# One-hot rows of eight tokens by one half-precision compare, in a product-key retrieval kernel

## The chip, the cores and the metric

The kernel runs on one core of a Trainium2 chip. The metric is the device time of one launch in microseconds (us). The engines are PE (TensorE: matmuls; PEld is its weight loads), DVE (VectorE), ACT (ScalarE), POOL (GpSimd) and SP (SyncE, which here only issues DMAs).

## The reference, cut to what matters

One encoder block on 1024 tokens of width 1024. The change lies in its last part, a retrieval with product keys (8 heads, 128 x 128 experts, the best 16 per head):

```
s = einsum('thpe,hpke->thpk', q, keys)          # two score rows of 128 per token and head
sv, si = top_k(s, 16)
cand = sv[:, :, 0, :, None] + sv[:, :, 1, None, :]
tv, ti = top_k(cand, 16)
eidx = (si0 * 128 + si1)[ti];  g = softmax(tv)
a = einsum('cd,ced->ce', x, utab[eidx])
out = einsum('ce,ced->cd', g * gelu(a), vtab[eidx])
```

## The kernel before, in words

The block runs as stages, each with its own set of engine programs; within a stage the engines meet only through semaphores, and the order of each engine's work is written out by hand. Three stages matter here.

**stage_select** picks the experts. For 6 of the 8 tiles of 128 tokens (the "dense" 768 tokens) PE turns three rows of 128 picks per token (first key number, second key number, gate share) into columns, and ACT copies them to `sel`, [128 picks, 3, 768 tokens]. Beside that PE computes `u @ utab.T` for 56 of the 128 expert rows (tiles), each as 48 matmuls of 384 columns in three float32 parts (`product3`, L79 to L81).

**stage_gates** does two things at once. It computes the other 72 tiles of `u @ utab.T` (`aps`; ACT puts them through gelu and stores them in `ahead`). And it scatters the gate shares into a dense table `gates[i, j, token]`. For a token, `second` is [128 picks, 128] with a one where the pick's second key number is j, and `first` is the same for i, times the share. One matmul of the two gives the token's 128 x 128 table. The share is kept as two half-precision parts, so there are two matmuls per token, 1536 in all (L1880). Tokens come in 192 groups of 4; the tables of a group fill one PSUM bank, which ACT copies out (`scatter_out`, L1899). In the program of PE a tile's 24 matmuls of the first half are followed by all groups of the tile but the last, and the second 24 by the last.

The one-hot rows are built per token by DVE from a half-precision row of column numbers, `iota`, as `tensor_scalar` compares: L1975 for `second`, L1980 for compare and share in one (twice, for tokens 0 and 1 of a group), L1977 for the bare compare of tokens 2 and 3, whose shares ACT then multiplies in (L1917, four per group, two groups ahead). There are four buffers, each for one group. DVE's program for a tile is: its groups (2 or 3), after each group one or two `dot`s (L1988, 1024 elements), and then `low` (L1993), which makes the low part of the next tile's `ut` and lets PE start that tile. The dots work on 256 expert rows that POOL gathers from DRAM into four slots (L1856); a slot is refilled when its dot is done. At the start SP loads the row of column numbers (L1838) and DVE prepares the shares (L1964 to L1968).

**stage_values** multiplies `ahead` by `gates`, splits the product and the rows of `vtab` into high and low parts, and accumulates 128 tiles of matmuls in groups of four (L79 to L81 with `va_` names). Its loads are issued by SP in program order (L2047 to L2062). `last_gates` are the semaphores of the three pieces in which the last block of `gates` is stored: rows 0 to 1, 2 to 7 and 8 to 127.

Of the kernel before, what the change touches and what calls it, by code (L numbers as in the profile page):

```python
# [8 lines left out]
F32 = mybir.dt.float32  # L9
F32R = mybir.dt.float32r  # L10
F16 = mybir.dt.float16
# [1536 lines left out]
SLOTS_G = 4  # L1548

# [10 lines left out]
def stage_select(nc, S, K, T):  # L1560
# [6 lines left out]
    with ctx:  # L1567
# [10 lines left out]
        iota = sb("iota", [P, TOPK])  # L1578
# [22 lines left out]
        def _(sp):  # L1601
            sp.dma_start(iota[:, :], T["iota"][0:TOPK].partition_broadcast(P)).then_inc(small, 16)
# [11 lines left out]
        def _(pool):  # L1614
# [10 lines left out]
            low(0, AT * KT)  # L1625

# [30 lines left out]
        def _(act):  # L1657
# [10 lines left out]
            def pair(i, dense):  # L1668
                for s in range(2):
# [29 lines left out]
        def _(dve):  # L1699
# [20 lines left out]
            def pair(i, dense):  # L1720
                for s in range(2):
# [24 lines left out]
                    for a in range(2):  # L1746
                        ch.link(v.tensor_tensor(hit[:, a, :, :], ab[:, a, :].unsqueeze(2).to_broadcast([P, PICKS, TOPK]),
                                                iota[:, :].unsqueeze(1).to_broadcast([P, PICKS, TOPK]), ALU.is_equal))
# [32 lines left out]
def stage_gates(nc, S, K, T):  # L1781
# [7 lines left out]
    with ctx:  # L1789
# [4 lines left out]
        iota32 = sb("iota32", [P, NK])  # L1794
        iota = sb("iota", [P, NK], F16)
        gh16 = sb("gh16", [P, DENSE], F16)
        gs = sb("gs", [P, 2, DENSE])
        first = sb("first", [P, 4, 2, G, NK], F16)
        second = sb("second", [P, 4, G, NK], F16)
# [10 lines left out]
        small, chain_s, f_ok, mm, act_out = (sem(n) for n in ("small", "chain", "f_ok", "mm", "act_out"))  # L1810
        shares_ok, hot_ok = sem("shares_ok"), sem("hot_ok")
# [6 lines left out]
        TURNS = 1  # L1818
        BY_ACT = (2, 3)
        TILES = BESIDE // TURNS  # L1820
        GROUPS = DENSE // G // TURNS
        ROWS = GATHERED * PICKS // TURNS
# [7 lines left out]

        def rows_after(b):
            return range(ROWS * b // GROUPS, ROWS * (b + 1) // GROUPS)

# [25 lines left out]
        def _(pe):  # L1859
            pe.sem_inc(mm, 4)  # L1860
            pe.sem_inc(a_mm, 4)
            for i in range(TURNS):
                for q in range(TILES):
                    n, s = TILES * i + q, q % 2
                    pe.wait_ge(ut_ok, n + 3)
                    todo = list(groups_of(q))
                    for h in range(2):
                        pe.wait_ge(gelu_ok, 2 * n + h + 1)
# [607 lines left out]
```

## Time and profile before

| | us |
|---|---|
| median of 3 runs | 4094.34 (4091.97 to 4097.99) |
| the profiled execution | 4094.17 |
| its span in the trace | 4092.4 |
| mean granted PE clock | 0.955 of full |

| engine | busy us | share of the span |
|---|---|---|
| PE | 3711.1 | 91% |
| DVE | 2666.7 | 65% |
| ACT | 1177.5 | 29% |
| POOL | 1195.0 | 29% |

The span runs from the first to the last instruction in the trace; the profiled execution's own time is 1.8 us more. Busy time of an engine is the union of its instructions' time. These are averages over stages with different limits: stage_gates lies at about 2150 to 2943 us of the span, stage_values behind it.

### The profile page before, as it was taken

What the parts mean: (1) busy time and instruction counts of PE and PEld (TensorE: products, weight loads), DVE (VectorE), ACT (ScalarE), POOL (GpSimd) and SP (SyncE); (2) the same over time, 40 slices, a digit from 0 to 9 for tenths busy, and PEclk for the clock granted to TensorE, in tenths of its full rate; (3) what the DMA queues carried; (4) which work ended last, traced back from release to release, by engine and by line L of the source; (5) the groups of instructions that cost most, each with busy time, mean ns of one, the idle gap of its engine ahead of it and who ended that gap; (6) DMA issues with size and microseconds to landing.
All of it is one profiled execution on the core that took longest, in us unless ns stands there. A gap on an engine that the chain in (4) does not pass through costs nothing. (4 is left out here: it accounts for less than half of the span.)

```text
span 4092.4 us, 54523 instructions
## 1 busy us (share of the span) xinstructions
PE 3711.1 (91%) x19170; PEld 3240.0 (79%) x19170; DVE 2666.7 (65%) x5849; ACT 1177.5 (29%) x2129; POOL 1195.0 (29%) x797
## 2 busy tenths in 40 slices
PE   5879899998887889899998999989679999999997
PEld 2579878886666778899998888888658888888875
DVE  4563033222555521699989999999767777777777
ACT  1110122221115221222335555556422222222220
POOL 1132112211332011233334343344333333333340
PEclk9789999998898989999999999999989999999998
DMA  4651212124545122333338999999988778888883
GB/s 174 262 194 36 88 59 74 71 76 155 201 159 185 67 86 78 115 129 121 131 112 276 310 327 311 327 315 325 309 283 291 286 282 293 290 291 294 290 292 112
DMA packets 502708, 826.52 MB, mean 202 GB/s; under 512 B 289175, under 2 KB 309911, under 8 KB 496440
## 3 DMA queue, kind: packets, MB, share of 16 engines
q1 hardware_dynamic: 111848, 370.03, 25.7%
q0 software_dynamic: 84096, 318.80, 21.4%
q10 hardware_dynamic: 306576, 135.28, 13.4%
q8 instruction: 105, 1.72, 0.2%
q14 instruction: 83, 0.68, 0.0%
HBM read 679.31 MB, written 144.70 MB: 201 GB/s over the span
## 5 line engine op out<-in xcount | busy, mean ns | idle before, releaser
L79 PE MATMUL va_fps<-va_vt_h,va_c_h 128*128 128x512 f32 x1536 | 608.1, 396 | 69.7 <-DVE va_vt_l L2210 36.0
L80 PE MATMUL va_fps<-va_vt_l,va_c_h 128*128 128x512 f32 x1536 | 605.7, 394 | 0.0
L81 PE MATMUL va_fps<-va_vt_h,va_c_l 128*128 128x512 f32 x1536 | 604.9, 394 | 0.0
L2088 POOL DMA_INDIRECT va_rows<-in_vtab,k_pick x256 | 396.5, 1549 | 657.9 <-DVE k_big L2234 572.8
L79 PE MATMUL ga_aps<-k_u_h,k_ut_h 128*128 128x384 f32 x1152 | 404.1, 351 | 13.9 <-DVE k_ut_l L1993 10.2
L79 PEld LDWEIGHTS va_fps<-va_vt_h,va_c_h 128*128 128x128 f32 x1536 | 293.4, 191 | 134.8 <-issue 38.4
L81 PE MATMUL ga_aps<-k_u_h,k_ut_l 128*128 128x384 f32 x1152 | 391.2, 340 | 0.0
L80 PE MATMUL ga_aps<-k_u_l,k_ut_h 128*128 128x384 f32 x1152 | 390.8, 339 | 0.0
L2234 DVE SCALAR_TENSOR_TENSOR k_big<-va_rows,va_coef,k_big 128x1024 f32<-128x1024 f32 x254 | 320.2, 1282 | 56.3 <-DMA va_rows<-in_vtab,k_pick 55.7
L80 PEld LDWEIGHTS va_fps<-va_vt_l,va_c_h 128*128 128x128 f32 x1536 | 293.6, 191 | 61.2
L81 PEld LDWEIGHTS va_fps<-va_vt_h,va_c_l 128*128 128x128 f32 x1536 | 293.1, 191 | 61.5
L1917 ACT ACTIVATE ga_first<-ga_first,ga_gs 128x128 f16<-128x128 f16 x768 | 245.6, 391 | 323.1 <-DVE ga_first L1977 323.1
L79 PE MATMUL se_aps<-k_u_h,k_ut_h 128*128 128x384 f32 x896 | 301.4, 336 | 15.5 <-POOL k_ut_l L1619 15.5
L2175 ACT ACTIVATE va_vt_h<-va_vt 128x1024 fp32r<-128x1024 f32 x128 | 135.3, 1057 | 577.4 <-PE va_fps L81 389.0
L80 PE MATMUL se_aps<-k_u_l,k_ut_h 128*128 128x384 f32 x896 | 300.8, 336 | 0.0
L81 PE MATMUL se_aps<-k_u_h,k_ut_l 128*128 128x384 f32 x896 | 300.6, 336 | 0.0
L1619 POOL TENSOR_TENSOR k_ut_l<-k_ut,k_ut_h 128x1024 fp32r<-128x1024 f32 x57 | 148.8, 2610 | 359.0 <-ACT k_ut_h L1666 359.0
L79 PEld LDWEIGHTS ga_aps<-k_u_h,k_ut_h 128*128 128x128 f32 x1152 | 220.8, 192 | 16.4 <-DVE k_ut_l L1993 12.2
L1856 POOL DMA_INDIRECT k_big<-in_urows,k_pick x128 | 171.3, 1338 | 193.1 <-DVE k_big L1988 174.5
L1856 POOL DMA_INDIRECT ga_rows<-in_urows,k_pick x128 | 145.8, 1139 | 279.7 <-DVE ga_rows L1988 264.9
L80 PEld LDWEIGHTS ga_aps<-k_u_l,k_ut_h 128*128 128x128 f32 x1152 | 220.7, 192 | 0.0
L81 PEld LDWEIGHTS ga_aps<-k_u_h,k_ut_l 128*128 128x128 f32 x1152 | 220.0, 191 | 0.0
(296 smaller groups left out, 8144.6 us busy)
## 6 DMA issues: line engine op xcount, KB each, us to landing
k_ut<-in_utab SPq DMA_DIRECT2D x129, 512.0 KB, 6.0
va_vt<-in_vtab SPq DMA_DIRECT2D x128, 512.0 KB, 6.9
va_c<-scratch_ahead SPq DMA_DIRECT2D x128, 384.0 KB, 3.4
va_wt<-scratch_gates SPq DMA_DIRECT2D x128, 384.0 KB, 5.1
hy_tab<-in_tab POOLq DMA_DIRECT2D x64, 512.0 KB, 4.8
scratch_ahead<-ga_gelu_a ACTq DMA_DIRECT2D x72, 384.0 KB, 5.7
sp_wada<-in_w_ada SPq DMA_DIRECT2D x24, 1024.0 KB, 8.6
scratch_gates<-ga_wide ACTq DMA_DIRECT2D x32, 768.0 KB, 12.1
```

Source lines behind the costliest of these rows:

```text
L79: nc.tensor.matmul(out, w[0], x[0], start=first, stop=False)
L80: nc.tensor.matmul(out, w[0], x[1], start=False, stop=False)
L81: return nc.tensor.matmul(out, w[1], x[0], start=False, stop=last)
L1619: nc.gpsimd.tensor_tensor(ut_l[:, s, :, :], ut[:, s, :, :], ut_h[:, s, :, :].bitcast(F32), ALU.subtract).then_inc(ut_ok, 1)
L1856: nc.gpsimd.indirect_dma_start(got[q % SLOTS_G], None, T["urows"], picked(K, q)).then_inc(got_in[q % SLOTS_G], 16)
L1917: last = nc.scalar.activation(first[:, b, part, t, :], first[:, b, 0, t, :], ACT.Copy, scale=gs[:, part, at:at + 1])
L2088: nc.gpsimd.indirect_dma_start(got[:, q % SLOTS_G, :], None, vrows, picked(K, q)).then_inc(got_in[q % SLOTS_G], 16)
L2175: nc.scalar.activation(vt_h[:, s, t, :], vt[:, t % 2, :], ACT.Copy).then_inc(vt_hi, 1)
L2234: v.scalar_tensor_tensor(out=sums[:, n, :], in0=got[:, k, :], scalar=share, in1=sums[:, n, :], op0=ALU.mult, op1=ALU.add).then_inc(row_use ...
```

## The change

In stage_select the first two rows of the turned picks go to `at16`, in half precision, and the share to `sel`, which is now [128, 768]. The column numbers 0 to 127 are loaded there once, and POOL writes them out as `iota16`, [128, 128 columns, 8 tokens], each number eight times in a row. stage_gates uses that: a batch is 8 tokens, `first` and `second` are stored as [columns, tokens], and DVE compares a whole batch in one `tensor_tensor` of 1024 elements for `first` and one for `second` (`hits`), and then multiplies in the two parts of the shares with two more (`weigh`, now on DVE). ACT no longer takes part. There are three buffers, each for one batch. PE's 1536 matmuls are the same in number and order, but read `first[:, b, part, :, t]` and `second[:, b, :, t]`: 128 half-precision numbers in steps of 8 elements, 16 bytes. DVE works up to two batches ahead of the tile.

In stage_values SP no longer loads `x1` at the start, and no longer waits for the third piece of the last gates before the loads of tiles 2 to 7; DVE waits for all three pieces before its first `turn` instead; POOL starts its gathers after two tiles are split.

```diff
@@ stage_select, gpsimd and scalar
+            pool.wait_ge(small, 16)
+            nc.gpsimd.tensor_copy(K["iota16"][:, :, :], K["iota"][:, :].unsqueeze(2).to_broadcast([P, NK, BATCH]))
...
-                    nc.scalar.activation(K["sel"][:, :, bass.ds((n - GATHERED) * P, P)],
-                                         tps[:, :].rearrange("p (a t) -> p a t", t=P), ACT.Copy).then_inc(t_ok, 1)
+                    at = bass.ds((n - GATHERED) * P, P)
+                    nc.scalar.activation(K["at16"][:, :, at], tps[:, 0:2 * P].rearrange("p (a t) -> p a t", t=P), ACT.Copy)
+                    nc.scalar.activation(K["sel"][:, at], tps[:, 2 * P:3 * P], ACT.Copy).then_inc(t_ok, 1)
@@ stage_gates
-        first = sb("first", [P, 4, 2, G, NK], F16)
-        second = sb("second", [P, 4, G, NK], F16)
+        SETS = 3
+        share16 = sb("share16", [P, 2, DENSE], F16)
+        first = sb("first", [P, SETS, 2, NK, BATCH], F16)
+        second = sb("second", [P, SETS, NK, BATCH], F16)
...
-            sp.dma_start(iota32[:, :], T["iota"][0:NK].partition_broadcast(P)).then_inc(small, 16)
@@ tensor
-                                    last = nc.tensor.matmul(ps[:, e, t * NK:(t + 1) * NK], second[:, e, t, :],
-                                                            first[:, e, part, t, :], start=part == 0, stop=part == 1)
+                                last = nc.tensor.matmul(ps[:, m % 4, t * NK:(t + 1) * NK], second[:, b, :, m * G % BATCH + t],
+                                                        first[:, b, part, :, m * G % BATCH + t], start=part == 0, stop=part == 1)
@@ scalar
-            def weigh(m):
...
-                        if m + AHEAD < BLOCKS * BLOCK:
-                            weigh(m + AHEAD)
@@ vector
-            def one_hot(m, b):
-                dve.wait_ge(mm, m + 1)
...
+            def hits(m):
+                if m >= SETS:
+                    dve.wait_ge(mm, 4 + BATCH // G * (m - SETS + 1))
+                b = m % SETS
+                v.tensor_tensor(first[:, b, 0, :, :], K["iota16"][:, :, :], of_batch(at16[:, 0, :], m), ALU.is_equal).then_inc(hot_ok, 1)
+                v.tensor_tensor(second[:, b, :, :], K["iota16"][:, :, :], of_batch(at16[:, 1, :], m), ALU.is_equal)
+
+            def weigh(m):
+                dve.wait_ge(hot_ok, m + 1)
+                b = m % SETS
+                for part in (1, 0):
+                    last = v.tensor_tensor(first[:, b, part, :, :], first[:, b, 0, :, :], of_batch(share16[:, part, :], m), ALU.mult)
+                last.then_inc(f_ok, 1)
...
+            for n in range(TILES):
+                for m in batches_of(n):
+                    if m:
+                        hits(m)
+                    for j in rows_after(m):
+                        dot(j)
+                    if m:
+                        weigh(m)
+                low(1 - n % 2, n + 1)
@@ stage_values, sync
-                sp.dma_start(x1[:, n, :], rows(S["x1"], order[n])).then_inc(x1_in[n], 16)
...
-            sp.wait_ge(K["last_gates"][1], 16)
-            sp.wait_ge(K["last_gates"][2], 16)
...
+            sp.wait_ge(K["last_gates"][1], 16)
+            for n in range(2, 8):
+                load(n % 2, n)
+            sp.wait_ge(K["last_gates"][2], 16)
@@ gpsimd and vector
+            pool.wait_ge(c_lo, 4)
...
+            for k in range(3):
+                dve.wait_ge(K["last_gates"][k], 16)
```

On DVE in the middle of stage_gates there stood, for a group of four tokens, its dots, and the start of the next group (`ga_first` and `ga_second` are the one-hot rows, `k_big` and `ga_rows` the slots of gathered rows):

```order
L1975 TENSOR_SCALAR ga_second<-ga_iota,k_sel 128x128
L1980 TENSOR_SCALAR ga_first<-ga_iota,k_sel,ga_gs 128x128 x2
L1975 TENSOR_SCALAR ga_second<-ga_iota,k_sel 128x128
L1980 TENSOR_SCALAR ga_first<-ga_iota,k_sel,ga_gs 128x128 x2
L1975 TENSOR_SCALAR ga_second<-ga_iota,k_sel 128x128
L1977 TENSOR_SCALAR ga_first<-ga_iota,k_sel 128x128
L1975 TENSOR_SCALAR ga_second<-ga_iota,k_sel 128x128
L1977 TENSOR_SCALAR ga_first<-ga_iota,k_sel 128x128
L1988 SCALAR_TENSOR_TENSOR k_big,k_dots<-k_big,k_u_row 128x1024 x2
```

Now, for a batch of eight tokens and the `low` behind it:

```order
L1957 TENSOR_TENSOR ga_first<-k_iota,k_at 128x1024
L1958 TENSOR_TENSOR ga_second<-k_iota,k_at 128x1024
L1977 SCALAR_TENSOR_TENSOR k_big,k_dots<-k_big,k_u_row 128x1024 x2
L1977 SCALAR_TENSOR_TENSOR ga_rows,k_dots<-ga_rows,k_u_row 128x1024
L1964 TENSOR_TENSOR ga_first<-ga_first,ga_share 128x1024 x2
L1982 TENSOR_TENSOR k_ut_l<-k_ut,k_ut_h 128x1024
```

Ten short instructions per four tokens have become four long ones per eight; the dots now stand between the compares and the products.

On SP at the start of stage_values (`va_c`, `va_wt` and `va_vt` are the tiles of `ahead`, `gates` and `vtab`) there stood:

```order
L2048 DMA va_c<-scratch_ahead 128x768
L2049 DMA va_vt<-in_vtab 128x1024
L2050 DMA va_x<-scratch_x 128x1024
L2048 DMA va_c<-scratch_ahead 128x768
L2049 DMA va_vt<-in_vtab 128x1024
L2050 DMA va_x<-scratch_x 128x1024
L2053 DMA va_wt<-scratch_gates 128x768 x2
L2068 UNCONDITIONAL_BRANCH
```

Now:

```order
L2039 DMA va_c<-scratch_ahead 128x768
L2040 DMA va_vt<-in_vtab 128x1024
L2039 DMA va_c<-scratch_ahead 128x768
L2040 DMA va_vt<-in_vtab 128x1024
L2043 DMA va_wt<-scratch_gates 128x768 x2
L2047 DMA va_c<-scratch_ahead 128x768
L2048 DMA va_wt<-scratch_gates 128x768
L2050 DMA va_vt<-in_vtab 128x1024
```

Two loads are gone from ahead of the first gates, and the loads of tiles 2 to 7 stand ahead of the loop, at whose entry (the branch) SP waited for the last two pieces.

## Rows read from the trace of the kernel before

**Rows 1.** Windows (us; busy time and instructions per engine, granted PE clock, DMA share, GB/s)

```profile
1700.00:2100.00 400.00, 400.00 (x2315) 399.82 (x2314) 374.81 (x1415) 119.10 (x169) 126.53 (x48) 1.00 0.36 129
2160.00:2940.00 780.00, 711.00 (x4947) 678.86 (x4948) 732.24 (x2490) 455.65 (x1168) 313.13 (x252) 0.99 1.08 314
```

**Rows 2.** Waits, 2160 to 2940: who waited for whom, us in total, times, longest

```profile
PE ga_ps L1880 <- ACT ga_first L1917: 61.9, 44, 3.7
...
PE ga_aps L79 <- DVE k_ut_l L1993: 10.2, 9, 2.9
DVE k_big L1988 <- DMA k_big<-in_urows,k_pick: 8.9, 8, 2.9
```

**Rows 3.** Timeline of DVE, one group of four tokens: start, us

```profile
2407.93 0.25 DVE L1975 TENSOR_SCALAR ga_second<-ga_iota,k_sel 128x128 f16<-128x128 f16 x1
...
2409.80 1.23 DVE L1988 SCALAR_TENSOR_TENSOR ga_rows<-ga_rows,k_u_row 128x1024 f32<-128x1024 f32 x1
2410.95 0.09 DVE L1988 DVE_READ_ACCUMULATOR ga_rows<-ga_rows,k_u_row 128x1 f32 x1
```

**Rows 4.** Instruction groups, 2160 to 2940: busy us, mean ns, idle before

```profile
L1917 ACT ACTIVATE ga_first<-ga_first,ga_gs 128x128 f16<-128x128 f16 x764 | 244.4, 391 | 311.5 <-DVE ga_first L1977 311.5
...
L1993 DVE TENSOR_TENSOR k_ut_l<-k_ut,k_ut_h 128x1024 fp32r<-128x1024 f32 x71 | 87.2, 1228 | 37.0 <-ACT k_ut_h L1894 36.8
```

**Rows 5.** Timeline of PE: one group's eight scatter matmuls

```profile
2407.64 0.62 PE L1880 MATMUL ga_ps<-ga_first,ga_second 128*128 128x128 f16 x8
```

**Rows 6.** One line's instructions, durations min/median/max: L1880, L981, L1312

```profile
L1880 PEld LDWEIGHTS ga_ps<-ga_first,ga_second x1536: 95/98/153, 2160.6 to 2942.8; 128*128 128x128 f16 x192
L1880 PE MATMUL ga_ps<-ga_first,ga_second x1536: 218/220/315, 2160.6 to 2942.8; 128*128 128x128 f16 x192
...
L981 PEld LDWEIGHTS hy_ps<-k_ident,k_big x64: 194/209/227, 1000.5 to 1125.3; 128*128 128x128 f32 x64
...
L1312 PEld LDWEIGHTS ou_tps<-k_ident,ou_row x64: 138/140/231, 1358.7 to 1434.0; 128*128 128x128 f32 x64
```

**Rows 7.** DVE groups of the whole span: short, strided and plain copies and sums

```profile
L560 DVE COPY k_qk<-pj_tps 128x128 f32<-128x128 f32 x80 | 22.8, 388 | 3.0 <-PE pj_tps L490 3.0
...
L1086 DVE TENSOR_TENSOR k_big<-k_big 128x512 f32<-128x512 f32 x16 | 11.1, 693 | 0.5
...
L1110 DVE TENSOR_TENSOR hy_prod<-hy_prod 128x512 f32<-128x512 f32 x8 | 5.5, 685 | 0.0
...
L557 DVE COPY k_qk<-pj_tps 128x256 f32<-128x256 f32 x8 | 3.3, 416 | 0.0
```

**Rows 8.** Timeline of DVE at the start of stage_gates

```profile
2153.89 0.23 DVE L1964 CAST ga_iota<-ga_iota 128x128 f16<-128x128 f32 x1 [15.67 <-DMA ga_iota<-in_iota]
```

**Rows 9.** Timelines of SP, DVE and PE at the start of stage_values

```profile
2951.60 1.05 SPq L2053 DMA_DIRECT2D va_wt<-scratch_gates  x2
2973.94 0.34 SPq L2059 DMA_DIRECT2D va_c<-scratch_ahead  x1
...
2965.97 0.96 DVE L2202 TENSOR_TENSOR va_c<-va_c,va_wt 128x768 f32<-128x768 f32 x1 [18.43 <-DMA va_wt<-scratch_gates]
...
2970.04 0.77 PE L79 MATMUL va_fps<-va_vt_h,va_c_h 128*128 128x512 f32 x1 [27.00 <-DVE va_vt_l L2210]
```

**Rows 10.** Windows around that start, as rows 1

```profile
2950.00:2960.00 10.00, 0.00 (x0) 0.00 (x0) 0.00 (x0) 1.06 (x1) 1.80 (x2) 0.50 1.00 368
2980.00:2990.00 10.00, 5.45 (x18) 4.04 (x18) 6.04 (x7) 3.69 (x4) 0.00 (x0) 0.83 0.73 253
```

**Rows 11.** DMA issues, 2940 to 3000: engine, KB each, us to landing

```profile
scratch_gates<-k_big ACTq DMA_DIRECT2D x1, 2880.0 KB, 28.8
```

**Rows 12.** DMA, 2160 to 2940: total, and one gather's time to landing

```profile
DMA packets 300766, 244.61 MB, mean 314 GB/s; under 512 B 250328, under 2 KB 250328, under 8 KB 300692
...
k_big<-in_urows,k_pick POOLq DMA_INDIRECT x126, 7.5
```

More of the change, by code:

```diff
@@ L1548 @@
 SLOTS_G = 4
+BATCH = 8
 def dense_half(h):
@@ new lines, in _ @@
+            for n in range(TILES):
+                s, todo = n % 2, list(groups_of(n))
+                pe.wait_ge(ut_ok, n + 3)
+                for h in range(2):
+                    pe.wait_ge(gelu_ok, 2 * n + h + 1)
+                    cut = dense_half(h)
+                    for k in range(KT):
+                        last = product3(nc, aps[:, 2 * s + h, 0:DH], (ut_h[:, s, k, :], ut_l[:, s, k, :]),
+                                        (u_h[:, k, cut], u_l[:, k, cut]), k == 0, k == KT - 1)
+                    last.then_inc(a_mm, 1)
+                    for m in (todo[:-1], todo[-1:])[h]:
+                        pe.wait_ge(f_ok, m * G // BATCH + 1)
+                        pe.wait_ge(act_out, m + 1)
+                        b = m * G // BATCH % SETS
+                        for t in range(G):
+                            for part in range(2):
+                                last = nc.tensor.matmul(ps[:, m % 4, t * NK:(t + 1) * NK], second[:, b, :, m * G % BATCH + t],
+                                                        first[:, b, part, :, m * G % BATCH + t], start=part == 0, stop=part == 1)
+                        last.then_inc(mm, 1)
@@ L1971, in one_hot @@
-            def one_hot(m, b):
-                dve.wait_ge(mm, m + 1)
-                for t in range(G):
-                    at = slice(m * G + t, m * G + t + 1)
-                    v.tensor_scalar(second[:, b, t, :], iota[:, :], K["sel"][:, 1, at], None, ALU.is_equal)
-                    if t in BY_ACT:
-                        last = v.tensor_scalar(first[:, b, 0, t, :], iota[:, :], K["sel"][:, 0, at], None, ALU.is_equal)
-                        continue
-                    for part in range(2):
-                        v.tensor_scalar(first[:, b, part, t, :], iota[:, :], K["sel"][:, 0, at],
-                                        gs[:, part, at], ALU.is_equal, ALU.mult)
-                last.then_inc(hot_ok, 1)
@@ new lines, in weigh @@
+            def weigh(m):
[4 more added lines that the diff above has]
+                last.then_inc(f_ok, 1)
+            hits(0)
+            ch.link(v.tensor_scalar(scaled[:, :], scaled[:, :], GATE_SCALE, None, ALU.mult))
+            ch.link(v.tensor_copy(share16[:, 0, :], scaled[:, :]))
+            ch.link(v.tensor_tensor(share16[:, 1, :], scaled[:, :], share16[:, 0, :], ALU.subtract))
@@ L1986, in dot @@
+            weigh(0)
+            def dot(j):
+                k, turn = j % SLOTS_G, j // SLOTS_G
                 dve.wait_ge(got_in[k], 16 * (turn + 1))
@@ L1994, in low @@
                                 ALU.subtract).then_inc(ut_ok, 1)
-            for i in range(TURNS):
-                for q in range(TILES):
-                    for b in groups_of(q):
-                        one_hot(GROUPS * i + b, b % 4)
-                        for j in rows_after(b):
-                            dot(i, j)
-                    low(1 - q % 2, TILES * i + q + 1)
+            for n in range(TILES):
+                for m in batches_of(n):
[6 more added lines that the diff above has]
+                low(1 - n % 2, n + 1)
 def stage_values(nc, S, K, T, out):
```

94 lines of the change are left out of this document (29 added, 65 removed).

## The prediction

> **What bounds the kernel now.** I read the windows first. In stage_select PE is busy for all of 400 us [rows 1]: 2315 matmuls, 0.173 us from one 384-column matmul to the next. In stage_gates it is busy for 711 of 780 us, and DVE for 732. So PE has some 69 us to win there. The waits say for what: 61.9 us for the one-hot rows of a group, which ACT finishes last, and 10.2 us for the low part of the next tile [rows 2]. ACT itself stood idle for 311.5 us waiting for DVE's compares [rows 4], so ACT is only the last link: DVE sets the pace. DVE's time for a tile, 780 / 72 = 10.83 us, can be added up. A group of four tokens takes 2409.80 - 2407.93 = 1.87 us of short compares, a dot 2410.95 - 2409.80 = 1.15 us [rows 3]. A tile has 2.67 groups, 3.56 dots and one `low`, which lasts 1.23 us and holds the engine for about as long as a dot [rows 4]: 4.99 + 4.09 + 1.15 = 10.2 us, and DVE's idle time of 780 - 732 = 48 us over 72 tiles is the other 0.67.
>
> PE's own need is 711 / 72 = 9.9 us per tile. It comes out of the pieces too: 48 x 0.173 = 8.3, and the other 1.6 us are 2.67 groups of 0.6 us each: eight scatter matmuls, 0.057 us from start to start ((0.62 - 0.22) / 7) [rows 5, 6], and the change-over.
>
> **The change, part by part.**
>
> *DVE in stage_gates.* Per eight tokens 3.74 us of short compares go, and four tensor_tensor of 1024 half-precision elements come. The trace has none such. Upper bound: as long as 1024 float32 elements, 1.15 us each. Lower bound, and the nearer row: as long as 512 float32 elements, which are the same number of bytes; they take 0.685 us alone [rows 7], 0.61 back to back if the 0.08 us by which a `low` overlaps its follower holds here too. I take 0.61, by bytes. A tile has 1.33 batches: 5.33 x 0.61 = 3.3, with dots and `low` 8.5 us, below PE's 9.9. At 1.15 it is 6.1 and 11.4 us. It crosses PE's 9.9 at 0.87 us per operation. The Trainium skill (Vector Engine (DVE) Microarchitecture Reference, section 5.1) says that a tensor_tensor whose operands all have two bytes and innermost step 1 takes two elements per cycle, also where one row is read again and again; no row here shows it.
>
> *ACT.* 768 activations go, 245 us off an engine that was busy for 456 [rows 1, 4]. Nothing waits longer for it; what gains is the 61.9 us of PE's wait.
>
> *PE.* Same matmuls, same order, but both operands are read in 16-byte steps. No row has that. The nearest: L981 loads 128 float32 columns in steps of 8 bytes (every second token) and takes 209 ns; L1312, the same transpose without steps, 140 [rows 6]. That is 0.54 ns more per column. A half-precision load takes only 98, so its reading goes another way, and loads hide under the matmul before them. How the moving read, which sets the 0.057, reacts, no row tells. Bounds: nothing, and the price of a new 16-byte line for each column. With 8-byte steps two columns share a line, and cost 2 x (0.417 + 0.54) = 1.9 ns (0.417 is one column at the full 2.4 GHz); one line per column would be 128 x 1.9 = 244 ns per matmul. For: DVE's copy of 128 elements into lines of their own (L560, steps of 1 KB) takes 388 ns where 256 plain ones take 416, about 1 ns more per element, and an 8-byte step costs DVE nothing (L1086 with steps, 693; L1110 without, 685) [rows 7]. Against: those are another engine's, and writes. I take nothing as the likeliest, because the two-byte operand asks for half of the bytes per column of the row that was slowed and I see no matmul spaced wider by a step; but this is the term on which everything hangs, and both ends stay. The Trainium skill (Advanced Engine Details and Errata, Memory Cachelines) speaks against the change: a 16-byte line must be hit at least twice to absorb the access time, and a new line at each access is penalised. Of its first half the trace disagrees for PE's loads: two hits per line were already slower, 209 against 140.
>
> *What PE wins.* With DVE at 8.5 us per tile the 61.9 us go; I leave the 10.2 for `low`. **-61.9 us.**
>
> *Start of stage_gates.* The load of the column numbers kept DVE idle until 2153.89 [rows 8]; it is gone, and the first batch is ready before PE's first 24 matmuls end. What PE loses by it lies mostly inside the 61.9, so I count nothing here. POOL writes the column numbers out after its last `low` in stage_select, under PE's last tile of 8.3 us: 1024 elements, for which its operations there took 126.53 / 48 = 2.6 us [rows 1]. Uncovered it would cost just that. ACT's second copy at the end of each dense tile is of 128 columns; its copies of 128 columns take 0.39 us [rows 4], once on the path to the next stage: nothing.
>
> *Start of stage_values.* PE stood for 27.0 us until the first tile was split, because the gates of that tile, issued at 2951.6, came at 2966.0; then again because the loads of tile 2, held by the last piece of the gates (2880 KB, 28.8 us), were issued only at 2973.9 [rows 9, 11]. The two loads of x1 and four gathers, 512 KB each, 3.1 MB, no longer share the way; at the 368 GB/s moved there [rows 10] they are 8.5 us. So the first tile comes some 8 us earlier. Tile 2's loads then leave about 2961, land within 7, and its part of PE's second stop (4.6 us of 2980 to 2990 [rows 10]) mostly goes: 3 more. The price if SP's loads collide instead: the 4.6 us stay and the first tile wins 5. **-11 us**, between -5 and -20. The gathers start later but are used only behind four tiles, and DVE's wait for the pieces ends before that.
>
> Sum against the profiled execution: 4094.2 - 61.9 - 11 = **4021 us**; its time is within 0.2 us of the median of the runs.
>
> **The rivals.** Each is 4021 plus a price.
>
> 1. *A step costs PE as in the row of 8 bytes.* 128 x 0.957 = 122 ns instead of 57, 1536 times: +100, **4121 us**. PE becomes the bound of its own accord, at 11.3 us per tile, and DVE's relief is worth nothing.
> 2. *Each column is a line of its own*, 244 ns: +287, **4308 us**, slower. The place is PE in stage_gates, and the spacing of the scatter matmuls decides: the gain is gone from 0.105 us on ((4094 - 4021) / 1536 + 0.057). The Trainium skill's rule on 16-byte lines, cited above, would give this case.
> 3. *DVE takes one element per cycle.* 11.4 us per tile instead of 10.2, nothing of the 61.9 is won: 4094.2 + 72 x 0.6 (over today's 10.83) - 11 = **4126 us**. Against it: the short compares already run 128 elements in 0.16 us.
> 4. *The transfers set it.* 244.6 MB in 718 us are 341 GB/s; the core moved 368 at the start of stage_values [rows 10, 12], so there is room. A slot's round is 780 / 64 = 12.2 us now and would have to be 11.2; issue 1.24 (313 / 252), landing 7.5 and dot 1.15 make 9.9, and DVE waited only 8.9 us for such a slot [rows 1, 2, 12]. If landings stretch and half is lost: **4052 us**.
>
> **How the numbers follow.** A measurement of this kernel tells a difference from none at about 0.2%, 8 us. Chances: forecast 0.48, and 0.05 for a step that costs less than the limit above; rival 1 0.22; rival 2 0.17; rival 3 0.04; rival 4 0.04. Faster: 0.48 + 0.05 + 0.04 = 0.57. Rival 1 touches "the same" where the step costs a little less than its row (102 to 110 ns), 0.08 of its 0.22. Slower: 0.14 + 0.17 + 0.04 = 0.35. The range goes down to 3990 (the 10.2 us of `low` and the larger gain at stage_values, 9 more, and some clock) and up to 4130, over rivals 1, 3 and 4; it leaves out rival 2. The forecast's own range is 3990 to 4050.
>
> **What would show it.** Right: the eight scatter matmuls of a group last 0.62 us as before; PE is busy for all but some 15 us of stage_gates, which lasts about 720; L1957, L1958 and L1964 take about 0.69 each and DVE is idle for 15% of the stage, waiting for buffers; ACT is busy for under 30% of it; from PE's last scatter matmul to its first matmul of stage_values there are 19 us instead of 27. Wrong: a group of eight that lasts 1.1 us (rival 1) or 2 us (rival 2), a load of L1882 well over 98 ns; tensor_tensor of 1.2 us (rival 3); waits of DVE for the gathered rows that make up tens of us (rival 4). If the second stop of PE in stage_values stays, the term of 11 us is wrong in its second part.

## The result, and the profile after

The changed kernel takes **4288.07 us** (median of 4 runs, 4285.92 to 4289.18) where the kernel before takes 4094.22 us beside it: the ratio is **1.0472, 95% interval 1.0454 to 1.049**. It is slower by 194 us. The forecast was 4021 us with a range up to 4130; rival 2 had said 4308.

The profiled execution (span 4286.3 us) says where. stage_gates, from its first matmul to the start of its last scatter matmul, goes from 2148.6 to 3148.1: 999.5 us where before it was 792.9. What lies behind that is 11.4 us shorter (1138.2 instead of 1149.6 to the end of the span). +206.6 - 11.4, and 1.3 us by which stage_gates starts earlier, make the 194.

The windows of stage_gates, with the columns of [rows 1]:

```profile
2160.00:3130.00 970.00, 958.50 (x4848) 818.96 (x4847) 609.07 (x957) 254.39 (x397) 357.78 (x251) 0.97 0.94 251
```

PE is busy for 99% of it, DVE for 63% instead of 94%, ACT for 26%; the same bytes now take longer, so the transfers fell from 314 to 251 GB/s. The waits of the same stretch say it too, against [rows 2]:

```profile
DVE ga_first L1957 <- PE ga_ps L1882: 350.1, 92, 8.7
...
PE ga_aps L79 <- DVE k_ut_l L1982: 11.5, 1, 11.5
```

The 61.9 us for one-hot rows are gone, and DVE now waits 350 us for PE. What PE does with the time stands in the scatter matmuls' own records and in the timeline of one batch, against [rows 5, 6]:

```profile
L1882 PEld LDWEIGHTS ga_ps<-ga_first,ga_second x1536: 142/146/168, 2154.5 to 3147.8; 128*128 128x128 f16 x192
L1882 PE MATMUL ga_ps<-ga_first,ga_second x1536: 405/413/442, 2154.5 to 3148.1; 128*128 128x128 f16 x192
```
```profile
2605.32 3.94 PE L1882 MATMUL ga_ps<-ga_first,ga_second 128*128 128x128 f16 x16
```

A load takes 146 ns instead of 98, a matmul 413 instead of 220, and sixteen of them start (3.94 - 0.41) / 15 = 0.235 us apart instead of 0.057. 1536 x 0.178 us are 273 us; some 60 us of waits that PE no longer has come off. DVE's share went as forecast: 1024 half-precision elements take the time of 512 float32 elements, 0.685 us alone (0.685 in [rows 7] too), and 0.61 us back to back (1.29 - 0.68; the pair of 1.29 us is in e1's timeline below).

```profile
L1964 DVE TENSOR_TENSOR ga_first<-ga_first,ga_share 128x1024 f16<-128x1024 f16 x190 | 122.4, 685 | 0.0
...
L1957 DVE TENSOR_TENSOR ga_first<-k_iota,k_at 128x1024 f16<-128x1024 f16 x94 | 65.1, 692 | 350.1 <-PE ga_ps L1882 350.1
L1958 DVE TENSOR_TENSOR ga_second<-k_iota,k_at 128x1024 f16<-128x1024 f16 x94 | 64.3, 685 | 0.0
```

The start of stage_values went as forecast as well (timelines, against [rows 9]): SP issues tile 2's loads 10 us after it asked for the first tiles' gates, where it had been 22. PE's gap is 18.42 us, not 27.00, and its second stop (4.55 us before) is 2.40.

```profile
3155.47 1.01 SPq L2043 DMA_DIRECT2D va_wt<-scratch_gates  x2
3165.73 0.33 SPq L2047 DMA_DIRECT2D va_c<-scratch_ahead  x1
...
3166.89 0.76 PE L79 MATMUL va_fps<-va_vt_h,va_c_h 128*128 128x512 f32 x1 [18.42 <-DVE va_vt_l L2204]
3179.53 0.50 PE L79 MATMUL va_fps<-va_vt_h,va_c_h 128*128 128x512 f32 x1 [2.40 <-DVE va_vt_l L2204]
```

### The profile page after: what moved, and what is told of

Read it like the earlier page. It is cut to its first block and busy times, and to the rows that moved or that the text cites. A ratio compares the mean times of both kernels' runs of the same rounds, so it can differ in the third digit from the quotient of the medians.

```text
span 4286.3 us, 52188 instructions
## 1 busy us (share of the span) xinstructions
PE 3975.4 (93%) x19170; PEld 3392.1 (79%) x19170; DVE 2544.9 (59%) x4311; ACT 980.1 (23%) x1367; POOL 1241.9 (29%) x798
## 5 line engine op out<-in xcount | busy, mean ns | idle before, releaser
L79 PE MATMUL ga_aps<-k_u_h,k_ut_h 128*128 128x384 f32 x1152 | 423.9, 368 | 15.2 <-DVE k_ut_l L1982 11.5
L1882 PE MATMUL ga_ps<-ga_first,ga_second 128*128 128x128 f16 x1536 | 387.2, 415 | 0.0
L1882 PEld LDWEIGHTS ga_ps<-ga_first,ga_second 128*128 128x128 f16 x1536 | 211.8, 147 | 127.6 <-issue 22.6
L1957 DVE TENSOR_TENSOR ga_first<-k_iota,k_at 128x1024 f16<-128x1024 f16 x96 | 66.5, 692 | 361.3 <-PE ga_ps L1882 350.1
L1860 POOL DMA_INDIRECT ga_rows<-in_urows,k_pick x128 | 177.0, 1383 | 350.7 <-DVE ga_rows L1977 314.9
L1860 POOL DMA_INDIRECT k_big<-in_urows,k_pick x128 | 187.4, 1464 | 255.9 <-DVE k_big L1977 226.3
```

Of the source, the lines that this page charges most:

```text
L79: nc.tensor.matmul(out, w[0], x[0], start=first, stop=False)
L1860: nc.gpsimd.indirect_dma_start(got[q % SLOTS_G], None, T["urows"], picked(K, q)).then_inc(got_in[q % SLOTS_G], 16)
L1882: last = nc.tensor.matmul(ps[:, m % 4, t * NK:(t + 1) * NK], second[:, b, :, m * G % BATCH + t], first[:, b, part, :, m * G % BATCH + t], ...
L1957: v.tensor_tensor(first[:, b, 0, :, :], K["iota16"][:, :, :], of_batch(at16[:, 0, :], m), ALU.is_equal).then_inc(hot_ok, 1)
```

## The experiments

Each is the kernel before or the changed one with the edit shown. e1, e2, e3 and e12 read other numbers than the one-hot rows, and e7 and e10 store the gates at another place in DRAM than the one they are read from, so these six compute a wrong result; counts and shapes stay. Stage lengths are taken as above, from the first matmul of stage_gates to the start of its last scatter matmul, in one profile each. PE's busy time and clock are those of the window 2160 to 2850.

| kernel | time, us | ratio to before, 95% interval | stage_gates | PE busy of 690 us | clock |
|---|---|---|---|---|---|
| before | 4094 | 1 | 792.9 | 632.2 | 0.98 |
| changed | 4288 | 1.0454 to 1.049 | 999.5 | 678.5 | 0.97 |
| e1, both reads plain | 4094 | 0.9996 to 1.002 | 803.5 | 624.7 | 0.96 |
| e2, moving read plain | 4100 | 1.0016 to 1.0047 | 813.6 | 641.0 | 0.95 |
| e3, loaded read plain | 4282 | 1.0456 to 1.0491 | 999.1 | 681.5 | 0.95 |
| e12, e3 with a 32-byte step | 4282 | one run | 999.2 | 682.4 | 0.96 |
| e4, pairs (4-byte step) | 4088 | 0.9996 to 1.002 | 807.3 | 631.7 | 0.96 |
| e5, low part early | 4060 | 0.9913 to 0.9961 | 767.8 | 651.3 | 0.97 |
| e6, dots spread | 4045 | 0.9875 to 0.9924 | 765.4 | 649.8 | 0.97 |
| e11, e6 with an 8-byte step | 4076 | 0.9956 to 0.9984 | 791.6 | 688.1 | 1.00 |
| e7, e4 with long packets | 4095 | 1.0005 to 1.004 | 810.5 | 622.3 | 0.95 |
| e10, e6 with long packets (two runs) | 3997 | 0.9741 to 0.9812 | 707.2 | 687.3 | 1.00 |
| e9, tile's store from SP | 4048 | 0.9884 to 0.9927 | 761.8 | 655.3 | 0.97 |
| e13, gates' stores from SP | 4041 | 0.986 to 0.9899 | 754.0 | 656.4 | 0.98 |
| e14, gates' stores from both | 4041 | 0.9862 to 0.9903 | 758.5 | 657.2 | 0.97 |
| e8, before, values' order alone | 4079 | 0.9973 to 1.0002 | 793.8 | 629.9 | 0.99 |
| e15, e6 with gates in blocks | **3986** | 0.975 to 0.9787 | 707.1 | 686.7 | 1.00 |
| e16, before, gates in blocks | 4062 | 0.9932 to 0.997 | 780.0 | 635.5 | 0.99 |

The kernel before took 4071 to 4105 us over the runs beside these; the ratios are to its runs on the same chip. In the profiles stage_gates starts anywhere between 2138 and 2157 us, also where all that lies ahead of it is the same, so of a difference between two profiles only what lies inside the stage that an edit touches is put down to it.

### Which read, and what a step costs: e1, e2, e3, e12

My theory: PE pays for a new 16-byte line in each column, in which of its two reads was open, and with plain reads the rest of the prediction comes true. The rivals stand in each expectation.

```diff
 # e1: both operands (j = the token's place in the batch); e2: the second only; e3: the first only
-second[:, b, :, j]
+second[:, b, 16 * j:16 * j + 16, :].rearrange("p n t -> p (n t)")
-first[:, b, part, :, j]
+first[:, b, part, 16 * j:16 * j + 16, :].rearrange("p n t -> p (n t)")
 # e12: e3, and the moving operand with every second column, out of both parts
-first[:, b, part, :, j]
+first[:, b, :, :, :].rearrange("p a (n z) t -> p a n (z t)", z=2)[:, :, :, j]
```

> The scatter matmuls read, out of the same buffers, 128 half-precision numbers that lie side by side (16 columns of 8 tokens) instead of every eighth number. They are not the one-hot rows, so the gates are other numbers; counts, shapes, order and waits are those of the changed kernel. Theory 'step' (the 16-byte step of PE's two reads is the whole loss; the rest of the prediction holds): the sixteen matmuls of a batch back at 0.057 us from start to start (0.62 us for eight), loads 98 ns, stage_gates some 720 us, time 4015 to 4035. Rival 'memory' (PE's reads are slow because DVE writes 1024-element rows beside them, or because the 2 KB of a batch lie together): spacing stays near 0.23 us and the time at 4288. Rival 'rest': the spacing is back, but DVE or the transfers then bound the tile at more than 9.9 us: 4050 to 4126.

> Only the moving operand is read side by side; the loaded one keeps its 16-byte step (the gates are other numbers again). Theory 'each pays' (load and moving read each pay a line per column and go one after the other): half of the 0.17 to 0.18 us that the spacing grew remains, spacing 0.14 us, time 4021 + 0.085 x 1536 = 4150. Theory 'moving' (only the moving read is on the path, a load hides under the matmul before it): spacing 0.057 to 0.07 us, time 4020 to 4040. Theory 'longer' (both take the same and overlap, the longer one counts): spacing stays at 0.23 us, 4288.

> The mirror of the run before: only the loaded operand is read side by side, the moving one keeps its 16-byte step. 'Each pays': spacing 0.14 us, 4150 us. 'Moving': spacing stays at 0.23 us, 4288 us, and the load's record goes from 146 back to 98 ns. 'Longer': also 4288. With the run before, the three theories give 4150 and 4150, 4030 and 4288, 4288 and 4288.

> The kernel of e3 (changed kernel, loaded operand side by side) with the moving operand read in steps of 32 bytes instead of 16: 64 columns from each of the two parts of a batch, so other gates. Theory 'a line per column' (16 bytes already give each column a line of its own; more can't cost more): spacing 0.224 us as in e3, 4280 us. Theory 'by the step': 0.4 us or more, 4550 or more.

The scatter matmuls' records of e1, e2 and e3, one fence each, then one group of eight of e3 and one of e12:

```profile
L1883 PEld LDWEIGHTS ga_ps<-ga_first,ga_second x1536: 96/98/103, 2151.9 to 2950.7; 128*128 128x128 f16 x192
L1883 PE MATMUL ga_ps<-ga_first,ga_second x1536: 218/220/232, 2151.9 to 2950.8; 128*128 128x128 f16 x192
```
```profile
L1883 PEld LDWEIGHTS ga_ps<-ga_first,ga_second x1536: 143/148/172, 2146.1 to 2953.8; 128*128 128x128 f16 x192
L1883 PE MATMUL ga_ps<-ga_first,ga_second x1536: 222/226/281, 2146.1 to 2953.8; 128*128 128x128 f16 x192
```
```profile
L1883 PEld LDWEIGHTS ga_ps<-ga_first,ga_second x1536: 97/116/118, 2149.0 to 3141.4; 128*128 128x128 f16 x192
L1883 PE MATMUL ga_ps<-ga_first,ga_second x1536: 387/405/408, 2149.0 to 3141.6; 128*128 128x128 f16 x192
```
```profile
2511.85 1.98 PE L1883 MATMUL ga_ps<-ga_first,ga_second 128*128 128x128 f16 x8
```
```profile
2510.99 2.01 PE L1883 MATMUL ga_ps<-ga_first,ga_second 128*128 128x128 f16 x8
```

It is the **moving read**. With it plain, the matmul is back at 226 ns although its load still takes 148; with only the load plain, the matmul stays at 405 and the kernel at 4282 us. The stepped load costs 50 ns in its own record, under the matmuls, and some 6 us of the whole (4100 against 4094 in e2 and e1, 4288 against 4282 in the changed kernel and e3; the stage of e2 is 10 us longer than that of e1). A 32-byte step costs what 16 bytes cost, within some 2% ((1.98 - 0.41) / 7 = 0.224 us in e3, (2.01 - 0.41) / 7 = 0.229 in e12), so it isn't the distance but the line per column that is paid.

But e1 and e2 also show a **second failed step**. With the reads mended the time should have been 4021; it is 4094 and 4100. PE's busy time is back, and so is its idle time. The waits of e1 and one place of its timelines (PE, DVE; 2160 to 2940):

```profile
DVE ga_first L1958 <- PE ga_ps L1883: 109.2, 44, 5.4
PE ga_aps L79 <- DVE k_ut_l L1983: 76.8, 24, 14.5
DVE ga_rows L1978 <- DMA ga_rows<-in_urows,k_pick: 42.0, 23, 3.9
```
```profile
2525.64 0.69 PE L79 MATMUL ga_aps<-k_u_h,k_ut_h 128*128 128x384 f32 x1 [5.05 <-DVE k_ut_l L1983]
...
2522.01 1.23 DVE L1978 SCALAR_TENSOR_TENSOR ga_rows<-ga_rows,k_u_row 128x1024 f32<-128x1024 f32 x1 [3.91 <-DMA ga_rows<-in_urows,k_pick]
2523.16 0.08 DVE L1978 DVE_READ_ACCUMULATOR ga_rows<-ga_rows,k_u_row 128x1 f32 x1
2523.16 1.29 DVE L1965 TENSOR_TENSOR ga_first<-ga_first,ga_share 128x1024 f16<-128x1024 f16 x2
2524.37 1.22 DVE L1983 TENSOR_TENSOR k_ut_l<-k_ut,k_ut_h 128x1024 fp32r<-128x1024 f32 x1
```

PE waits 5.05 us for the next tile's low part; DVE does it last in a tile, behind a dot product that waited 3.91 us for its gathered row. DVE is idle for a fifth of the stage and late all the same. In the changed kernel PE is slow enough for everybody, and only one such wait shows, 11.5 us, at the start.

### Pairs, and the order of DVE's work: e4, e5, e6, e11

A layout of four pairs of tokens keeps DVE's single compare and gives PE steps of 4 bytes:

```diff
 # e4
-first = sb("first", [P, SETS, 2, NK, BATCH], F16)
-second = sb("second", [P, SETS, NK, BATCH], F16)
+first = sb("first", [P, SETS, 2, BATCH // STEP, NK, STEP], F16)      # STEP = 2
+second = sb("second", [P, SETS, BATCH // STEP, NK, STEP], F16)
-second[:, b, :, j], first[:, b, part, :, j]
+second[:, b, j // STEP, :, j % STEP], first[:, b, part, j // STEP, :, j % STEP]
 # e5: e4, and
     hits(m)
+    if m == batches_of(n)[0]: low(1 - n % 2, n + 1)
     for j in rows_after(m): dot(j)
     weigh(m)
-low(1 - n % 2, n + 1)
 # e6: compare, low, dot, compare, dot, product, dot, product: one dot behind each, as far as there are dots
 # e11: e6 with STEP = 4
```

> The same one compare for eight tokens, but the buffers hold pairs of tokens: [four pairs, 128, 2], so PE reads in steps of 4 bytes, four columns to 16 bytes. By the row of 8-byte steps of before (0.54 ns more per column of a load), halved for half the step: 0.27 x 128 = 35 ns more per matmul, +54, 4075 us. If what counts is only whether a 16-byte line is hit once, the step costs nothing: 4021. If any step sends a read down another way: 0.23 us, 4288. For DVE the innermost run is then 2 elements: it takes 0.69 us as now if length of the run doesn't matter, 1.15 or more if it does, and then DVE bounds the tile at 11.4 us or more: 4126 and up. The Trainium skill (Advanced Engine Details and Errata, Memory Cachelines) says that a line has to be hit at least twice; by that rule this kernel pays nothing for its steps.

> In e1 and e4 PE no longer waits for the one-hot rows but for the next tile's low part: 70 to 74 us in 22 to 25 waits, where the kernel before had 62 + 10. The kernel of e4 with one thing moved: DVE computes the next tile's low part right behind the first compare of a tile instead of behind all its batches. Theory 'order' (the low part is late because it stands behind a compare that waits for a buffer of PE's and behind three dot products that wait for gathered rows): the wait falls from 74 to under 20 us and the time from 4088 to 4025 to 4045. Theory 'transfers' (at 314 to 319 GB/s the DMA engines are full in stage_gates in every version, so whatever gets rid of one wait finds another): the waits change their names, the stage stays at 800 us, time 4080 to 4090.

> As the run before, and the two or three dot products of a batch no longer stand together: one behind each of the batch's four compares and products. Theory 'bursts' (a gathered row's place is freed three at a time, POOL then issues three gathers one behind the other, 1.3 us each, and the last lands too late): DVE's waits for gathered rows fall from 50 to 60 us to under 15, as with the even spacing of the kernel before (8.9), and the time is 10 to 30 us below e5, 4015 to 4030. Theory 'transfers': DVE's waits for rows stay above 40 us and the time is within 5 us of e5.

> The kernel of e6 with quads of tokens instead of pairs: PE reads in steps of 8 bytes, two columns to 16 bytes. The nearest row of before, a load of 128 float32 columns in steps of 8 bytes, took 69 ns more than one without. Theory 'any line hit twice is free' (that row is slow for its four-byte numbers): spacing 0.057 us, load 98, time as e6, 4045. Theory 'by the step' (the price grows with the step between 4 bytes, where e4 pays nothing, and 16, where it is 0.17 us): spacing 0.09 to 0.12 us, +50 to +100 us on PE, time 4060 to 4130. The Trainium skill (Advanced Engine Details and Errata, Memory Cachelines) has two hits per line as enough.

One group of eight of e4, then of e11:

```profile
2506.49 0.65 PE L1884 MATMUL ga_ps<-ga_first,ga_second 128*128 128x128 f16 x8
```
```profile
2509.01 1.11 PE L1884 MATMUL ga_ps<-ga_first,ga_second 128*128 128x128 f16 x8
```

**4 bytes cost PE nothing** (0.060 us apart), **8 bytes 0.116 us** ((1.11 - 0.30) / 7), 16 and 32 bytes 0.22 to 0.24. Per column that is 0.47, 0.9 and 1.8 ns: one 16-byte line in about 1.8 ns, shared by as many columns as lie in it. With four in a line that comes to 0.45 ns, as much as a column takes in a plain read (0.057 us / 128), so nothing is left to pay. The Trainium skill (Advanced Engine Details and Errata, Memory Cachelines) says that at least two hits on a line absorb the access. For one hit the measurement agrees. For two it doesn't: e11 pays 0.056 us for each of 1536 matmuls, 86 us of PE's time; its stage is only 26 us longer than e6's, because PE no longer has e6's waits (38 us of 690) and its clock is 1.00 instead of 0.97. DVE does not mind runs of two elements: 0.69 us as before.

e4 ends at 4088, the time of the kernel before, so it isn't the step alone. e5 and e6 move nothing but DVE's order. PE's wait for the low part (2160 to 2850) goes 66.3, 36.3, 37.0 us; DVE's waits for gathered rows 49.0, 74.8, 33.9. The order was worth 40 us of stage. The spreading won 15 us of time by the medians, but the stage that it touches is only 2 us shorter, so its worth isn't shown. Both are less than I had expected (PE's wait under 20 us, the rows' under 15). What is left of PE's wait has changed its cause. ACT's and DVE's waits of e6, and a piece of ACT's timeline:

```profile
ACT k_ut_h L1898 <- issue: 136.6, 32, 8.0
DVE k_ut_l L1993 <- ACT k_ut_h L1898: 100.9, 28, 8.1
PE ga_aps L79 <- DVE k_ut_l L1993: 37.0, 14, 5.6
```
```profile
2458.34 0.45 ACTq L1912 DMA_DIRECT2D scratch_gates<-k_big  x1
...
2464.19 7.20 ACTq L1930 DMA_DIRECT2D scratch_ahead<-ga_gelu_a  x1
2471.49 1.06 ACT L1898 ACTIVATE k_ut_h<-k_ut 128x1024 fp32r<-128x1024 f32 x1 [6.73 <-issue]
```

ACT issues a piece of the gates in 0.45 us and then stands for 7.20 us at the issue of the next store; its rounded copy, DVE's low part and PE stand behind it.

### Queue or transfers: e7, e9, e10, e13, e14

Every piece of the gates is 4096 runs of 192 bytes in DRAM (32 columns of 128 partitions; the 12,288 in e9's expectation was a slip). Is it these packets, and do they fill a queue or the DMA engines? In e7 and e10 SP also waits for all three last pieces before it loads the first gates; in e13 and e14 it issues its pieces between its loads of the next tiles (`k_ut`).

```diff
 # e7: e4 and e10: e6, the same bytes in another place
-act.dma_start(S["gates"].rearrange("i j t -> j i t")[:, lo:hi, block * TW:(block + 1) * TW], ...)
+act.dma_start(S["gates"].rearrange("i j t -> i (j t)")[:, at + lo * TW:at + hi * TW].rearrange("p (i t) -> p i t", t=TW), ...)
 # e9: e6, the store of the finished tile from SP
-act.dma_start(S["ahead"][n + FIRST], gelu_a[:, a, :])
+sp.dma_start(S["ahead"][bass.ds(n + FIRST, 1)][0], gelu_a[:, a, :])
 # e13: e6, the gates' pieces from SP; e14: every second piece
-act.dma_start(S["gates"]..., wide...)
+sp.dma_start(S["gates"]..., wide...)
```

> The kernel of e4, but the gates are stored with each partition's 32 x 48 numbers side by side (6 KB) instead of in 32 pieces of 192 bytes; the same bytes, in another place, so the values are summed with other gates. stage_values waits for all three last pieces before its first gates are read, which costs some 15 to 20 us once. It tests the transfers alone: their queue (q10 of the page) holds 47.7% of the 16 engines' time in stage_gates for 73 of 243 MB. Theory 'transfers': gathers land in 6 us instead of 7.8, PE's wait for the low part falls from 74 to under 25 us, stage_gates from 800 to 740 us; the time 4045 to 4055. Theory 'order': the wait stays above 50 us, the stage at 780 to 800 us, the time at 4090 to 4105.

> The kernel of e6 with the gates stored in 6 KB pieces as in e7 (another place, so other gates are summed; stage_values waits for all three last pieces). In e7 ACT's issues never lasted more than 0.35 us, but DVE was late by its order. Theory 'queue': with the order mended and short packets gone, both waits are gone: ACT for 'issue' under 10 us, PE for the low part under 10 us, stage_gates 25 to 45 us shorter than in e6; the whole 3990 to 4025, some 15 of it for the wait for the pieces. Theory 'order is all': nothing more to win, PE still waits some 40 us, 4045 to 4060.

> In e6 PE still waits 42.6 us for the next tile's low part, because DVE waits 103 us for ACT's rounded copy, and ACT waits 144 us for nothing but its own sequencer: its issue of the store of a finished tile took up to 8.9 us (median 2.3; in the kernel before 0.34). The kernel of e6 with that store issued by SyncE instead, between its loads of the next tiles. Theory 'queue' (the issue stands behind the 12,288 short packets of a stored piece of gates in ScalarE's own queue, and everything behind it on ScalarE is late): ACT's waits for 'issue' fall under 20 us, PE's for the low part under 10, the granted clock of the stage rises from 0.97 to 0.99, time 3985 to 4010. Theory 'transfers' (the issue is slow because the 16 DMA engines are full): SyncE's issues become as slow, PE's waits stay at 35 us or more, time 4035 to 4050.

> The kernel of e6 with all pieces of the gates (but the last block's) issued by SyncE, so that ScalarE issues only the store of the finished tile. In e6 and e9 ScalarE's own issues blocked it for 100 to 144 us, whichever store stood second; in e10, with long packets, for 5. Theory 'queue' (what blocks is that ScalarE waits at its issue while its queue is full; the transfers themselves have room): ScalarE's waits for 'issue' fall under 15 us, SyncE's issues of a piece last up to 10 us and cost nothing, PE's waits for the low part fall from 42.6 under 15 us, time 4005 to 4025. Theory 'transfers' (the 192-byte packets fill the 16 engines, whoever issues them): ScalarE waits instead for a block's stores before it writes the next one, or DVE for gathered rows; PE's waits stay above 30 us, 4040 to 4055.

> As the run before, but every second piece from SyncE and the others from ScalarE. Theory 'queue': two queues are each half as full, no issue of either lasts over 1 us, a piece lands in 10 to 16 us; PE's waits for the low part under 10 us, time 4000 to 4020, a little better than e13. Theory 'transfers': as e6 within 5 us, 4040 to 4050.

e7 alone would have misled: long packets took the DMA share from 1.06 to 0.86 and won nothing, because DVE's order held PE at the same place (67.7 us of wait). With the order mended, e10 loses PE's wait but for 2.2 us and is 58 us shorter in the stage than e6. So the two causes lay one behind the other: from e4 on, the order alone won 40 us of the stage, the packets alone nothing, both together 100.

The remedy of "queue", another issuing engine, failed in three runs. In e9 the block moved on to the gates' own issues on ACT (up to 9.9 us), in e13 to SP's loads (first row below), for which ACT then waited (second row), and in e14 both engines were held, ACT for up to 11.4 us at the tile's store and SP for up to 6.3 at a load; all three end at 4041 to 4048, as e6.

```profile
L1847 SPq DMA_DIRECT2D k_ut<-in_utab x71: 328/6373/14481, 2148.0 to 2868.9; - x71
```
```profile
ACT k_ut_h L1915 <- DMA k_ut<-in_utab: 101.2, 32, 8.5
```
```profile
2160.00:2850.00 690.00, 656.43 (x4574) 633.01 (x4573) 565.28 (x894) 226.39 (x375) 274.23 (x238) 0.98 1.10 331
```

With DVE's order mended and short packets, e5, e6, e9, e13 and e14 have a DMA share of 1.10 to 1.11 (the third row is e13's; the share sums the packets' times, so it can pass 1); e10 and e15, with long ones, 0.95 to 0.96. That they move 354 to 356 GB/s and the others 326 to 331 says no more than the stages' lengths, since the bytes are the same. The Trainium skill (DMA: Bandwidth & Descriptors, Rules for kernel authors) says that spreading transfers over issuing engines brings no bandwidth; e13 and e14 agree.

So it is shown that the short packets cost e6 its 58 us, and that moving them between ACT and SP doesn't help. It is not shown that they fill the 16 engines. The traces speak rather for the hold at the issue: what was held was always on an engine that itself issued short packets (SP's longest issue in e9, which issues none there, is 0.63 us; ACT's in e13 is 0.40), and in all these runs something urgent stands behind it on that engine. The gathers of the same stretch hardly feel the packets: in the median they land in 7.2 to 7.9 us in e4, and in 6.7 to 7.5 in e7. A run in which an engine issues the short packets and nothing that anybody waits for was not made.

### A version with the right result: e15, and the parts alone: e8, e16

```diff
 # e15: e6, and e16: the kernel before, both with
-dram("gates", (NK, NK, DENSE))
+dram("gates", (DENSE // 48, NK, NK, 48))
-act.dma_start(S["gates"].rearrange("i j t -> j i t")[:, lo:hi, block * TW:(block + 1) * TW], ...)
+act.dma_start(S["gates"][block, :, lo:hi, :], ...)
-sp.dma_start(wt[:, s, :], S["gates"][bass.ds(n, 1)][0])
+sp.dma_start(tile_of(wt, s), S["gates"].rearrange("b j i t -> i j b t")[bass.ds(n, 1)][0])
 # e8: the kernel before with the change's stage_values alone
```

> e13 and e14 stayed at 4041 whichever queue carried the short packets: the 16 DMA engines are full with them. This is the kernel of e6 with the gates laid out in DRAM as [block of 48 tokens, j, i, token]: the same values, stored in pieces of 6 KB per partition and, in stage_values, read in packets of 192 bytes. Theory 'transfers': stage_gates becomes as in e10, some 36 us shorter than in e6 (708 us, clock 1.00); the short packets' time, 22% of 16 engines over 710 us, moves to stage_values (14% of its 1137 us, where the share is 0.80), which stays under 1. If it hides there: 4000 to 4015. Rival: the loads of gates in stage_values land later (5 us become 8 or more), its tiles wait, 20 us or more are given back: 4025 to 4060.

> The kernel before with this other layout of the gates alone. There DVE's and ACT's one-hot rows bound the tile, not the transfers. If that is so, stage_gates gains nothing (PE still waits some 60 us for the rows): 4085 to 4095 with a little more or less at stage_values. If short packets already held it back: 4050 to 4070.

> The kernel before, with the third part of the change alone: the order of loads at the start of stage_values, the gathers behind four tiles, DVE's waits for the last pieces. By the prediction's term and by the changed kernel (PE's gap 18.4 us instead of 27.0, no second stop of 4.6) it is worth 11 us: 4094 to 4083. If the gap closed only because stage_gates ended otherwise, it stays at 4094.

```profile
2160.00:2850.00 690.00, 686.72 (x4889) 664.21 (x4889) 602.44 (x954) 249.72 (x400) 290.32 (x250) 1.00 0.95 354
2950.00:3950.00 1000.00, 978.26 (x4291) 808.00 (x4290) 767.53 (x721) 217.58 (x239) 365.91 (x236) 0.99 0.87 284
```

e15 takes **3986 us, 2.3% less than the kernel before**. stage_gates is at PE's own need (x4889 in 686.7 us, one wait of 2.2). The short packets are now read in stage_values, where the share rises from 0.81 (e6) to 0.87 and PE loses nothing (978 us busy of 1000, e6 973). It is 14 us below the range that I expected. The stage came out at the 708 us of the expectation, but that is 58 us less than in e6 and not the 36 that I had put into the sum. Part of it is the clock, 1.00 instead of 0.97. PE's records show this as busy time: 649.80 / 4512 = 0.1440 us a matmul in e6, 686.72 / 4889 = 0.1405 here.

e16 was a miss: I expected nothing, it won 0.5% (19 us by the medians; its profile is 13 us shorter in stage_gates and 14 behind it, and another 11 us ahead of it, which the edit doesn't touch). PE's wait for the rows stayed (54.5 us of 690, before 53.5), so DVE sets that kernel's pace as read; but PE's wait for the low part, 7.4 us there before, is gone. The last piece of the gates (2880 KB) lands in 10.1 us instead of 28.8; how the 14 us behind stage_gates come about I did not follow up.

e8: the time doesn't settle it (0.9973 to 1.0002, centre -5 us). In its trace the gap is 19.90 us instead of 27.00, the second stop 0.36 instead of 4.55, and what lies behind stage_gates is 7.7 us shorter (1141.9 instead of 1149.6).

## Why the prediction was wrong

*What bounds the kernel now* was right as far as it went: DVE sets the pace, PE's own need is 9.9 us per tile. e15 runs at 707.1 / 72 = 9.8.

*DVE in stage_gates*: right. 0.61 us per operation by bytes. The Trainium skill (Vector Engine (DVE) Microarchitecture Reference, section 5.1) has two elements per cycle for it; the 685 ns, as for half as many float32 elements, agree.

*PE*: **the step "I take nothing as the likeliest" failed, and by it the verdict.** The bound was good: a line per column, worked out as 0.244 us from the transpose's load, measured 0.235. So was rival 1's: 0.122 at 8 bytes, measured 0.116. That my price came so near is in part luck: it was worked out from a float32 load, and this kernel's own half-precision load at the same 16-byte step lasts 146 ns, not 244. The reason I gave for "nothing", that a two-byte operand asks for half of the bytes per column, counts bytes where these runs show that lines count. The row of the 8-byte step (209 against 140 ns) was the only one that I had of PE's own reads with a step; it was slowed, and nothing spoke for 16 bytes being better. Its price belonged in the sum, and "nothing" among the rivals.

*What PE wins*: **the step "with DVE at 8.5 us per tile the 61.9 us go" failed too**, and would have cost the forecast by itself: 4094 (e1) instead of 4021. The wait for the one-hot rows went, and where 10.2 us of wait for the low part had been there were now 76.8 (e1, 2160 to 2940). It was an argument from averages. Eight tokens at once make DVE's work lumpy: a compare that waits for a buffer of PE's (109 us), then three dot products one behind the other whose rows come back singly, then the low part on which PE stands. I left the 10.2 us of `low` as they were and did not ask what stands ahead of it. Rival 4 was right that the transfers would matter, but not how: the same bytes went at 356 GB/s in long packets (e10), and it was the 192-byte packets that cost. That its 4052 lies where the kernels with mended order ended (4041 to 4060) is luck.

*ACT*: the 245 us went, and nothing waited for them: right.

*Start of stage_gates*: the load is gone, but PE stood 11.5 us for the second tile's low part, which DVE does behind the first tile's batches; I had counted nothing.

*Start of stage_values*: right. 11.4 us where 11 were forecast; the gap 18.42 where 19 were.

## What to carry to other kernels

A layout that makes one engine's instruction long and plain puts steps into another engine's reads: price the moving operand of a matmul by the 16-byte lines that it touches, and keep four half-precision columns in a line (a layout in pairs of tokens, a 4-byte step, did, at no cost to DVE). When an engine is relieved, ask what it now does in one piece, and what small, urgent operation stands behind that piece. A wait that survives its repair may have a second cause behind the first: try both together before dropping either.

## What the runs showed of the hardware

- A matmul's moving read in half precision takes about 1.8 ns per 16-byte line: a matmul of 128 columns starts 0.060 us after the one before at a 4-byte step (e4), 0.116 at 8 (e11), 0.224 to 0.235 at 16 and 32 (e3, e12, the changed kernel).
- A load of 128 half-precision columns takes 146 to 148 ns at a 16-byte step instead of 98 (117 at 8 bytes), hidden under matmuls; a plain load takes 116 when the moving read beside it is stepped (e3).
- On an engine that also issues transfers in 192-byte packets, an issue can hold it for up to 14.5 us (e13), and it isn't always the issue of the short packets that is held. The issues of the engine that issued none stayed under 0.7 us (SP in e9, ACT in e13).
- The granted clock over 2160 to 2850, of which 1.00 is the 2.4 GHz level, was 0.95 to 0.97 where PE stood 33 to 68 us (e1, e2, e4 to e7, e9, e14), but 0.98 in e13, where it stood 34, and in the kernel before, where it stood 58; it was 1.00 in e10 and e15, where PE stood 3 us. With 16-byte steps it is 0.97 although PE's records leave no gap, and with 8-byte steps 1.00, as the same window of the changed kernel and of e11 shows; why is open:

```profile
2460.00:2560.00 100.00, 100.00 (x504) 85.42 (x503) 63.50 (x101) 26.22 (x41) 38.16 (x26) 0.97 0.91 256
```
```profile
2460.00:2560.00 100.00, 100.00 (x638) 96.84 (x637) 73.96 (x117) 32.93 (x53) 37.32 (x31) 1.00 1.16 309
```
